# First attention's keys and values in column halves, pieces of products between the heads, and another order of the recurrence's units

## The reference

```
# layer 0: gated recurrence
u = rmsnorm(x) @ w_in                    # 1024 -> 2048
gate, rec = u[..., :1024], u[..., 1024:]
rec = causal_depthwise_conv(rec)         # 4 taps
r, i = sigmoid(per-block matmul of rec)  # 8 blocks of 128 -> 256
a = exp(-8 r softplus(-lam));  b = sqrt(1 - a*a) * (i * rec)
h_t = a_t h_{t-1} + b_t                  # scan over positions
x = x + (gelu(gate) * h) @ w_out
x = x + sqrelu_mlp(rmsnorm(x))
# layer 1: banded attention, 16 heads of 64
k, v = rmsnorm(x, kv_norm) @ w_kv        # k: another rmsnorm per head
q = rmsnorm(x, b_norm) @ w_q             # and one per head
o = softmax(q k / 8 + relative bias, masked) v
x = x + o @ w_o;  x = x + sqrelu_mlp(rmsnorm(x))
```

## Time and profile before

| what | us |
|---|---|
| three runs | 1095.34, 1095.55, 1096.88 (median 1095.55) |
| the profiled execution, its own time | 1094.01 |
| its span on the core | 1092.1 |
| PE busy | 1037.0 (95%) |
| DVE busy | 652.5 (60%) |
| ACT busy | 567.1 (52%) |
| POOL busy | 120.1 (11%) |
| keys' first product to `score(0)` | 316.98 to 384.17 |
| `score(0)` to the last output unit | 384.17 to 454.72 |

### The profile page before, as it was taken

One profiled execution on the slowest core, in us unless ns is written; L12 is line 12 of the kernel. 1 busy time (PEld: TensorE's weight loads), 2 busy tenths in 40 slices (PEclk: granted clock), 3 DMA queues, 4 the chain that ended last, 5 costly groups with the idle time before them and its releaser, 6 DMA issues. The chain is left out here.

```text
span 1092.1 us, 16410 instructions
## 1 busy us (share of the span) xinstructions
PE 1037.0 (95%) x6694; PEld 929.1 (85%) x6694; DVE 652.5 (60%) x881; ACT 567.1 (52%) x854; POOL 120.1 (11%) x118
## 2 busy tenths in 40 slices
PE   5887999999999989999999989999999979999997
PEld 5886799999988856699899979988899869999996
DVE  5658675555567755575555564365654657676764
ACT  6586464444446455464444454455544356556652
POOL 3555110000000011330000000000001510000000
PEclk9999999999999969999999999999999989999999
DMA  9643567555545431375556527543344625655520
GB/s 314 197 155 123 185 225 238 192 177 190 175 138 205 163 108 39 121 231 192 189 192 192 181 94 226 173 136 117 101 131 131 216 78 193 196 190 193 193 78 38
DMA packets 117970, 180.40 MB, mean 165 GB/s; under 512 B 3113, under 2 KB 93577, under 8 KB 117913
## 3 DMA queue, kind: packets, MB, share of 16 engines
q1 hardware_dynamic: 116099, 174.16, 48.7%
q0 software_dynamic: 1696, 5.39, 1.5%
q10 hardware_dynamic: 118, 0.05, 0.0%
HBM read 178.48 MB, written 1.10 MB: 164 GB/s over the span
## 5 line engine op out<-in xcount | busy, mean ns | idle before, releaser
L996 PE MATMUL PS<-XA,whi 128*128 128x256 f32 x2576 | 473.1, 286 | 8.2 <-DVE XA L1472 5.0
L1421 DVE TENSOR_TENSOR wlo<-raw,whi 128x2048 fp32r<-128x2048 f32 x153 | 351.5, 2304 | 170.4 <-ACT whi L605 166.1
L996 PEld LDWEIGHTS PS<-XA,whi 128*128 128x128 f32 x2576 | 407.2, 193 | 18.7 <-issue 14.5
L605 ACT ACTIVATE whi<-raw 128x2048 fp32r<-128x2048 f32 x158 | 301.4, 1912 | 148.4 <-PE PS L1041 117.5
L996 PE MATMUL PS<-XA,wlo 128*128 128x256 f32 x1288 | 366.4, 284 | 0.0
L996 PEld LDWEIGHTS PS<-XA,wlo 128*128 128x128 f32 x1288 | 248.8, 193 | 0.0
L1041 PE MATMUL PS<-whi,XB 128*128 128x512 f32 x800 | 226.7, 391 | 1.0 <-DVE XB L1683 1.0
L1041 PEld LDWEIGHTS PS<-whi,XB 128*128 128x128 f32 x800 | 147.6, 188 | 29.9 <-issue 1.7
L1041 PE MATMUL PS<-wlo,XB 128*128 128x512 f32 x400 | 127.5, 390 | 0.0
L1041 PEld LDWEIGHTS PS<-wlo,XB 128*128 128x128 f32 x400 | 75.2, 188 | 15.8
L1041 PE MATMUL PS<-whi,XA 128*128 128x512 f32 x256 | 73.7, 396 | 10.0 <-DVE XA L1553 8.4
(11 more groups left out here) (207 smaller groups left out, 1013.2 us busy)
## 6 DMA issues: line engine op xcount, KB each, us to landing
raw<-in_w_up SPq DMA_DIRECT2D x32, 1024.0 KB, 5.5
raw<-in_w_down SPq DMA_DIRECT2D x32, 1024.0 KB, 4.9
raw<-in_w_ffn_up SPq DMA_DIRECT2D x22, 1024.0 KB, 5.1
raw<-in_w_in SPq DMA_DIRECT2D x21, 1024.0 KB, 5.2
raw<-in_w_ffn_down SPq DMA_DIRECT2D x11, 1024.0 KB, 4.9
raw<-in_a_w_in SPq DMA_DIRECT2D x8, 1024.0 KB, 8.5
raw<-in_w_kv SPq DMA_DIRECT2D x8, 1024.0 KB, 6.1
raw<-in_w_mem_kv SPq DMA_DIRECT2D x4, 1024.0 KB, 5.2
```

What stands on the lines that cost most here:

```text
L605: act.activation(whi[:, s, :], raw[:, s, :], ACT.Copy).then_inc(s_hi, 1)
L996: ins = pe.matmul(PS[:, bank_of(g), 0:T], w[:, k, P * m:P * m + P], X[:, k0 + k, part, :], start=(i == 0 and part == 0 and w is hi), stop= ...
L1421: dve.tensor_tensor(wlo[:, s, :], raw[:, s, :], whi[:, s, :].bitcast(F32), ALU.subtract).then_inc(s_lo, 1)
```

## The change

**Recurrence.** The units come as rec 0 to 3, gate 0, the gate matrices, gate 1, gate 2, gate 3, and the memory's. Gate units are evacuated by plain copies, and two gelus over 1024 columns each follow later. The low part of the convolved input is DVE's. POOL keeps its product of i and rec. The scale and scan steps are interleaved with the splits.

**First attention.** Keys and values are made in column halves: two units of 512 rows by 512 columns each for heads 0 to 7 (`U_K`, `U_V`) before the heads, and two each for heads 8 to 15 (`U_K1`, `U_V1`) in 16 pieces between the heads' steps, with the 12 pieces of the output product: 28 pieces, 1 to 3 a head (`FILL`). The norm per head runs in four rounds of 512 columns (keys 0, queries 0, queries 1, keys 1), the root as a power over 16 columns on POOL. Seven units are split in halves by ACT and by DVE within the heads. POOL subtracts nothing any more.

```diff
-U_REC, U_GATE, U_LRU = [0, 1, 3, 5], [2, 4, 6, 7], 8
+U_REC, U_GATE, U_LRU = [0, 1, 2, 3], [4, 6, 7, 8], 5
-U_K, U_Q, U_V, U_O = 49, 53, 57, 61
+U_K, U_Q, U_V, U_K1, U_V1, U_O = 49, 51, 55, 57, 59, 61
...
-        SPLIT_AT = {5: U_O, 9: U_O + 1, 13: U_O + 2}
+        FILL = [3, 3, 2, 1, 1, 1, 2, 2, 1, 2, 2, 2, 2, 1, 2, 1]
+        SPLIT_AT = {0: U_K1, 1: U_K1 + 1, 3: U_V1, 6: U_V1 + 1, 9: U_O, 11: U_O + 1, 13: U_O + 2}
...
@@ gpsimd
-            for u in POOL_SPLIT_MEM:
-                split(u)
...
-            for u in POOL_SPLIT_O:
-                split(u)
+            for r in range(4):
+                pool.wait_ge(s_ms, r + 1)
+                link(pool.tensor_scalar(kss[:, r % 2, :], kss[:, r % 2, :], EPS, 0.0, ALU.add, ALU.add))
+                pool.tensor_tensor(krs[:, r % 2, :], kss[:, r % 2, :], mhalf[:, 0:16], ALU.pow).then_inc(s_rms, 1)
@@ scalar
             rec_unit(0)
             rec_unit(1)
             conv_hi(0)
             act.wait_ge(s_ew, 32)
-            gate_unit(0)
+            rec_unit(2)
             conv_hi(1)
-            rec_unit(2)
-            gate_unit(1)
+            rec_unit(3)
             conv_hi(2)
             squares(SQ_NORM[1], xn, lambda i: act.wait_ge(s_mem, 16))
-            rec_unit(3)
-            gate_unit(2)
+            split(U_GATE[0] + LEAD)
             conv_hi(3)
-            gate_unit(3)
+            gate_out(0)
             for n in range(8):
...
             split(U_LRU + LEAD)
+            decay(0)
+            split(U_GATE[1] + LEAD)
+            gate_out(1)
+            decay(1)
             norm_hi(1, [(XB, R_MEM)], bank=4)
+            split(U_GATE[2] + LEAD)
+            gate_out(2)
...
+            split(U_GATE[3] + LEAD)
+            gate_out(3)
...
             unit_b(U_Q)
-            kq_square(0)
+            kq_square(KQ_K0)
             unit_b(U_Q + 1)
-            kq_root(0)
             unit_b(U_Q + 2)
-            kq_evac(0)
             unit_b(U_Q + 3)
+            kq_evac(KQ_K0)
+            kq_square(KQ_Q0)
             unit_b(U_V)
-            kq_square(1)
+            kq_square(KQ_Q1)
             unit_b(U_V + 1)
...
+            kq_evac(KQ_Q0)
...
             exps(0)
             exps(1)
-            values_out()
+            values_out(U_V, 0)
             for H in range(16):
+                if H in SPLIT_AT:
+                    split(SPLIT_AT[H] + LEAD, part=0)
                 if H + 2 < 16:
                     exps(H + 2)
+                probs_out(H)
                 if H:
                     attn_hi(H - 1)
+                if H == 1:
+                    kq_evac(KQ_Q1)
+                if H == 4:
+                    kq_square(KQ_K1)
+                if H == 5:
+                    kq_evac(KQ_K1)
+                if H == 8:
+                    values_out(U_V1, 1)
                 if H in SPLIT_AT:
+                    split(SPLIT_AT[H] + LEAD, part=1)
@@ tensor
+            for i in range(1, 4):
+                unit_a(U_REC[i], G_REC[i])
+            unit_a(U_GATE[0], G_GATE[0])
             have(U_LRU)
...
+            unit_a(U_GATE[1], G_GATE[1])
             pe.wait_ge(s_lru, 8)
             norm_T(1, bank=4)
+            unit_a(U_GATE[2], G_GATE[2])
+            unit_a(U_GATE[3], G_GATE[3])
...
+            def half_columns(u, i, X, k):
+                t_banks = KV_BANKS[u]
+                hi, lo = W4(whi, (u + i) % SLOTS), W4(wlo, (u + i) % SLOTS)
+                for t in range(TT):
+                    for part_, w in ((0, hi), (0, lo), (1, hi)):
+                        ins = pe.matmul(PS[:, t_banks[t], :], X[:, 4 * i + k, part_, P * t:P * t + P], w[:, k, :],
...
+                if i == 2:
+                    kq_T(KQ_K0)
...
+            def fill(j):
+                if j < 16:
+                    u, i, k = (U_K1, U_V1)[j // 8], j // 4 % 2, j % 4
+                    if j == 0:
+                        pe.wait_ge(s_vev, 2)
+                    if j == 8:
+                        pe.wait_ge(s_kqev, 6)
...
             for H in range(16):
+                if H == 6:
+                    pe.wait_ge(s_kqev, 8)
                 if H + 2 < 16:
                     score(H + 2)
+                for j in range(FILL_FROM[H], FILL_FROM[H + 1]):
+                    fill(j)
+                if H == 1:
+                    kq_T(KQ_Q1)
+                if H == 5:
+                    kq_T(KQ_K1)
                 probs_T(H)
@@ vector
+            split(U_K + LEAD)
+            split(U_K + 1 + LEAD)
...
             split(U_Q + LEAD)
+            kq_out(KQ_K0, U_K + 1, (4, 6))
+            split(U_Q + 1 + LEAD)
+            kq_sum(KQ_K0)
+            split(U_Q + 2 + LEAD)
+            kq_scale(KQ_K0)
+            split(U_Q + 3 + LEAD)
+            kq_out(KQ_Q0, U_Q + 3, (5, 7))
+            kq_out(KQ_Q1, U_Q + 3, (0, 1))
+            kq_sum(KQ_Q0)
+            kq_scale(KQ_Q0)
+            split(U_V + LEAD)
+            kq_sum(KQ_Q1)
+            kq_scale(KQ_Q1)
+            split(U_V + 1 + LEAD)
...
             for H in range(16):
                 norm_probs(H)
                 if H == 0:
+                    values_out(U_V, 0)
                 if H + 2 < 16:
                     row_max(H + 2)
                 if H:
                     attn_lo(H - 1)
+                if H == 3:
+                    kq_out(KQ_K1, U_K1 + 1, (4, 6))
+                if H == 4:
+                    kq_sum(KQ_K1)
+                    kq_scale(KQ_K1)
+                if H == 8:
+                    values_out(U_V1, 1)
+                for part in range(2):
+                    if H - part in SPLIT_AT:
+                        split(SPLIT_AT[H - part] + LEAD, part=part)
```

More of the change, by code:

```diff
@@ L705, in conv_hi, with gate_out, decay @@
                     act.activation(XB[:, k, 0, :], xc[:, k, :], ACT.Copy).then_inc(s_ch, 1)
-            def gate_unit(i):
-                unit_a(U_GATE[i], G_GATE[i], [gate[:, 2 * i + m, :] for m in range(2)], ACT.Gelu_apprx_tanh)
+            def gate_out(i):
+                for m in range(2):
+                    evac(G_GATE[i] + m, BEFORE(U_GATE[i]) + m + 1, gate[:, 2 * i + m, :])
+            def decay(h):
+                act.wait_ge(s_lru, 8)
+                act.wait_ge(s_cc, 1)
+                for n in range(4 * h, 4 * h + 4):
+                    act.activation(av[:, n, :], rg[:, n, :], ACT.Exp, scale=cneg[:, n:n + 1]).then_inc(s_a, 1)
+                for n in range(4 * h, 4 * h + 4):
+                    act.activation(rg[:, n, :], rg[:, n, :], ACT.Tanh, scale=cpos[:, n:n + 1]).then_inc(s_a, 1)
             rec_unit(0)
@@ L747, in _ @@
                 act.activation(rg[:, 4 * h:4 * h + 4, :], rg[:, 4 * h:4 * h + 4, :], ACT.Sqrt).then_inc(s_sq, 1)
-            split(U_MEMK + 1 + LEAD)
+            split(U_GATE[3] + LEAD)
+            gate_out(3)
+            for h in range(2):
+                v = gate[:, 4 * h:4 * h + 4, :]
+                act.wait_ge(s_evac, G_GATE[2 * h + 1] + 2)
+                act.activation(v, v, ACT.Gelu_apprx_tanh).then_inc(s_gelu, 1)
+            for h in range(2):
+                split(U_MEMK + h + LEAD)
+                for m in range(2):
+                    evac(G_MEMK + 2 * h + m, BEFORE(U_MEMK + h) + m + 1, kT_me[:, 2 * h + m, :])
             split(U_MEMV + LEAD)
@@ L1196, in _ @@
-            layer_b(U_Q, XB, bank=0, pieces_=False, ready=lambda i: kq_T(0) if i == 3 else None)
-            pe.wait_ge(s_kqev, 4)
-            for i in range(3):
-                have(U_V + i)
-                tokens((U_V + i) % SLOTS, W2, 2, XA, 2 * i, 4, 2, i == 0, False)
-            kq_T(1)
-            have(U_V + 3)
+                        for part_, w in ((0, hi), (0, lo), (1, hi)):
+                            for c in range(2):
+                                ins = pe.matmul(PS[:, Q_BANKS[t][c], :], XB[:, 2 * i + k, part_, P * t:P * t + P],
+                                                w[:, k, 512 * c:512 * c + 512],
+                                                start=(i == 0 and k == 0 and part_ == 0 and w is hi),
+                                                stop=(i == 3 and k == 1 and part_ == 1), skip_group_check=True)
@@ L1404, in link, with split @@
                 dve.wait_ge(s_chain, chain[0])
-            def split(u, it=0, units=0):
+            def split(u, it=0, units=0, part=None):
                 if u is None or u >= N_UNITS:
@@ L1554, in y_lo, with scan @@
                                   XA[:, 4 * k:4 * k + 4, 0, :].bitcast(F32), ALU.subtract).then_inc(s_yl, 1)
-            dve.wait_ge(s_evac, G_GATE[3] + 2)
-            for h in range(2):
+            def scan(h):
                 dve.wait_ge(s_sq, h + 1)
@@ L1566, in _, with y_out @@
                 link(ins)
+            def y_out(h):
+                dve.wait_ge(s_gelu, h + 1)
                 dve.tensor_tensor(half(xc, h), half(rg, h), half(gate, h), ALU.mult).then_inc(s_y, 1)
+            scale2(0)
+            split(U_GATE[1] + LEAD)
+            scale2(1)
```

(25 more changed lines are left out.)

251 lines of the change are left out of this document (116 added, 135 removed).

## The result

The changed kernel takes 1106.63 us (median of 4 runs, 1105.2 to 1109.67) beside 1096.22 (median of 4, 1095.34 to 1097.11) for the kernel before in the same measurement: a ratio of 1.0099, 95% interval 1.0075 to 1.0122. It is slower by 1.0%, which is over the 0.2% that a measurement tells apart. The profiled execution took 1109.67, the slowest of the four, with a span of 1106.1.

A forecast was written before the change was run, and what follows sets the result against it. TensorE, busy 95%, bounds the kernel; only its idle and slow stretches can be won. Attention 10.4 us longer, recurrence 7.7 shorter: +2.7, so 1096.7 beside the profile's 1094.0, 1098.3 beside the 1095.55 median; range 1089 to 1108, own 1094 to 1102.

The forecast's parts named there:

- third rival: Key and query norms: POOL's power goes by column; at 3 us each 9.8 us more, 1108.1; chance 0.25.
- Recurrence, 7.7 less: Recurrence: 16.6 us of idle and clock loss before, 8.9 after (2.3 + 4.3 + 2.3), a gain of 7.7.
- Keys to score 0, 55.6: First attention up to score 0: 46.4 us of work plus 1.25, 5.6 and 2.3 added, against 67.19 before.
- Heads, 92.5: First attention's heads: 75.0 us of work, 15.15 of waits and 2.3 of half clock, against 70.55 before.
- Piece 0's wait of 3.05: Start of the heads: DVE's last split, maximum, exps, norm and first values' evacuation delay piece 0 by 3.05 us.
- the second key half's 3.3: Head 5: PE's key transposes wait 3.3 us for evacuation, square, sum, POOL's power and scaling.
- score 8: In the heads, score 8 waits 1.95 us for the evacuation of the second key half.
- the unknown price: POOL's 16-column power in four chains: taken as 0.56 us, bounds 0.56 to 9.0; each microsecond more costs 4.
- The second key half is hidden: Rival in the heads: its chain is done by the end of head 5's piece; 8.45 us go, 1089.9; chance 0.22.
- The clock holds: Rival in the attention: full clock after the 5.6 and 3.3 us waits; 4.6 us less, 1093.7; chance 0.08.
- The recurrence gains nothing: Rival in the recurrence: the new wait is as long as the old; 1106.0; chance 0.03.
- gain of 3.43 us and of some 8.4 of half clock: Heads 0 to 4: removing POOL's subtraction wins PE's 3.43 us wait and some 8.4 us of half clock behind it.

The follow-up runs named there:

- pow_col: Changed kernel with POOL's power on one column of 16 and a memset of 1.0 for the others: 1098.38 us, ratio to before 1.0022.
- no_pool_heads: Kernel before with the four weight subtractions that POOL does around the heads moved to DVE: 1090.11 us against 1097.9, ratio 0.9928.

## Why the prediction was right, and where it was not

It had the sign, the mechanism and the wide range (1089 to 1108). Its likeliest number, 1098.3, was 8.3 us short, and the time lies outside the range that it gave to its own forecast (1094 to 1102) and 1.4 us inside the wide one: it is its third rival that came. By its own steps:

- **Recurrence, 7.7 less; measured 9.3.** Gate unit 0 waited 2.27 us (forecast 2.3), the gate blocks 4.00 (4.3) until 56.69, at half clock until 60.4 (61.6), with no wait before the output product, which began at 103.63 (103.8). The moves were right, and so was what PE waited for. The sum of waits gave less than its own arrival time does: 110.68 - 103.8 + 1.96 of lost clock is 8.8.
- **Keys to score 0, 55.6; measured 58.78.** The wait before the first transposes was 7.53 for 5.6. With the power at the assumed price it was 5.34, and the stage 55.26.
- **Heads, 92.5; measured 101.77.** Small waits came where they were put: 1.15, 0.88 and 1.23 us for 1.05, 0.95 and 1.25 in heads 2 to 4; 0.74 for 0.7 at head 9. Piece 0's wait of 3.05 came as 6.02 + 1.03, the second key half's 3.3 as 5.47; score 8 had 0.93 for 1.95, and the 0.9 at head 5's probabilities did not come. With the cheap power the first pair was 2.31 + 1.75, the key wait 3.30, and the stage 95.96. Of the 3.5 us still missing, 0.6 are idle time (15.8 for 15.15, with 3.2 for 2.0 at the end) and 2.9 PE's busy time (80.2 for 77.3): this stage has two stretches at half clock, 10.2 us, where one was forecast.
- **The mis-sized term** is the unknown price. The prediction bounded POOL's power at 16 columns between 0.56 and 9.0 us and took 0.56, because the only row of the operation was at one column. It measured 2.92, 2.36 us more in each of four chains, and `pow_col` shows what that costs: 8.3 us by the two medians, 9.3 in the traces of the attention. "It stands in four chains, so each microsecond more costs 4" came out in size, but not chain by chain: PE waited for three of them in full and for the first query half's 0.44 us, and half clock made up the rest. The rival at 3 us (1108.1, chance 0.25; its 4 x 2.4 = 9.8 is 4 x 2.44) is what happened. The traces held a hint, though no proof: 0.56 us for a power of one column on an engine whose addition of one column took 0.30 (L477 before), and whose subtraction of 2048 columns takes 4.54 (2.2 ns a column). So some 0.26 us looked like the power's own, by estimate 4 us at 16 columns if they are paid for each, and the end where the price doesn't grow was not the safe one to take.
- **What offset what.** That the number for the cheap power came within 0.1 us of `pow_col`'s 1098.38 is luck in part: the recurrence gained 1.6 us more than forecast, the attention lost 3.1 more (151.22 for 148.1) even with the cheap power, and the kernel before was 1 us slower in that measurement.
- **Rivals.** "The second key half is hidden" is out: its transposes waited 5.5 us, and 3.3 with the cheap power. "The clock holds" is out: three stretches at 0.50. "The recurrence gains nothing" is out: it gained 9.3.
- **The clock.** Each of the three long waits went with half clock, and filling the waits returned about 3.4 us for 23.9 less at half: the price of the clock was small there. The Trainium skill, "TensorE: Matmul & The Clock Gate", section "HAM oscillation", has the clock go back to half after idle gaps; these three rows agree. But a gap is not needed: `no_pool_heads` has 17.1 us at half in heads 0 to 4 with no wait over 1.21 us. So the prediction's gain of 3.43 us and of some 8.4 of half clock behind them had the wait right and the clock's cause wrong. (By its own pace five heads and a piece are 5 x 2.06 + 1.5 = 11.8 us and not 10.9; the term is not in the sum.) In the changed kernel, with pieces of 512 columns in those heads, the stretch ended at 381.21, 7.8 us behind the wait, for 19.27 before; no run changes the pieces alone.

## What to carry to other kernels

When an operation is widened, price it from two widths, or assume that what is dear at one column is dear at each; and multiply an unknown price by the number of chains that it stands in before choosing an end. An idle engine is not free: both of POOL's roles here, the large subtraction that holds DVE up and the small link in a chain, cost more than the same work on engines at 51 to 60%. Edits that give nothing one by one may need each other: test them in pairs before dropping them.
